# Who issues the blanking of one block of result rows: SyncE in place of ScalarE

## The reference

```
proj = x @ w_in
...
mix = jnp.concatenate([y_pool, y_conv], axis=-1) @ w_out
x = layer_norm(DEEPNORM_ALPHA_3 * x + mix, ln1_g, ln1_b)
ffn = moe(x, router_w, router_b, w_gate_up, b_gate_up, w_down, b_down)
```

## Time and profile before

| | before |
|---|---|
| median of 3 runs | 3319.97 us (3319.68 to 3324.28) |
| the profiled execution | 3321.52 us |
| its span, first to last instruction | 3319.7 us |
| TensorE busy | 94% of the span |
| VectorE, ScalarE, GpSimd busy | 55%, 48%, 22% |
| bytes moved | 693.72 MB, 209 GB/s over the span |
| the mixer stage | about 1800 to 1948 us |

### The profile page before, as it was taken

One profiled execution on the slowest core, in us unless ns is written; L12 is line 12 of the kernel. 1 busy time (PEld: TensorE's weight loads), 2 busy tenths in 40 slices (PEclk: granted clock), 3 DMA queues, 4 the chain that ended last, 5 costly groups with the idle time before them and its releaser, 6 DMA issues. The chain is left out here.

```text
span 3319.7 us, 39152 instructions
## 1 busy us (share of the span) xinstructions
PE 3104.9 (94%) x14036; PEld 2408.6 (73%) x14036; DVE 1830.9 (55%) x2216; ACT 1596.4 (48%) x2141; POOL 737.2 (22%) x379
## 2 busy tenths in 40 slices
PE   7986999998999999989997888999999999999997
PEld 6754678877877787768885666777777777777753
DVE  3257433344367404440031447887888888888773
ACT  4334434433566423232231325766766766666652
POOL 2400144442523344324442330000000000000020
PEclk9987999999999999999998898999999999999998
DMA  3243322222222132212224317999999999999971
GB/s 148 102 161 119 127 76 101 101 89 89 77 76 76 52 114 77 102 51 101 89 108 191 153 51 318 402 408 411 406 407 412 405 408 411 406 407 411 411 262 45
DMA packets 65594, 693.72 MB, mean 209 GB/s; under 512 B 6912, under 2 KB 7296, under 8 KB 25440
## 3 DMA queue, kind: packets, MB, share of 16 engines
q1 hardware_dynamic: 54336, 650.05, 49.8%
q0 software_dynamic: 6912, 25.17, 2.0%
q10 hardware_dynamic: 4256, 17.30, 1.3%
HBM read 654.22 MB, written 38.27 MB: 209 GB/s over the span
## 5 line engine op out<-in xcount | busy, mean ns | idle before, releaser
L142 POOL TENSOR_TENSOR ring_low<-ring,mix_ring_high 128x1024 fp32r<-128x1024 f32 x120 | 292.4, 2470 | 455.2 <-ACT mix_ring_high L137 455.2
L213 PE MATMUL psum<-mix_high,mix_ring_high 128*128 128x512 f32 x864 | 342.9, 397 | 13.1 <-DVE h_low L507 8.6
L215 PE MATMUL psum<-mix_high,ring_low 128*128 128x512 f32 x864 | 337.1, 390 | 0.0
L213 PE MATMUL psum<-ex_high,ex_rows_high 128*128 128x512 f32 x768 | 314.9, 410 | 1.5 <-DVE ex_rows_low L2823 1.4
L215 PE MATMUL psum<-ex_high,ex_rows_low 128*128 128x512 f32 x768 | 299.7, 390 | 0.0
L214 PE MATMUL psum<-h_low,mix_ring_high 128*128 128x512 f32 x736 | 287.2, 390 | 0.0
L142 POOL TENSOR_TENSOR ring_low<-ring,ff_ring_high 128x1024 fp32r<-128x1024 f32 x72 | 175.0, 2464 | 415.0 <-ACT ff_ring_high L137 224.7
L2510 POOL CAST ex_index<-table 128x1 uint32 (+1 forms) x32 | 5.9, 184 | 1090.2 <-PE psum L2550 1032.5
L2854 DVE TENSOR_TENSOR ring_low<-ring,ex_high 128x2048 fp32r<-128x2048 f32 x96 | 214.4, 2287 | 38.7 <-ACT ex_high L2686 38.6
L2854 DVE TENSOR_TENSOR ex_more_low<-ex_more,ex_high_in_x 128x2048 fp32r<-128x2048 f32 x96 | 219.5, 2287 | 19.9 <-ACT ex_high_in_x L2686 19.9
L2605 PE MATMUL psum<-ex_more,ex_act_t 128*128 128x512 f32 x512 | 224.9, 592 | 0.0
(11 more groups left out here) (581 smaller groups left out, 6884.8 us busy)
## 6 DMA issues: line engine op xcount, KB each, us to landing
ex_more<-moe_w SPq DMA_DIRECT2D x128, 2048.0 KB, 9.3
ring<-wstream SPq DMA_DIRECT2D x87, 2048.0 KB, 8.4
ring<-moe_w SPq DMA_DIRECT2D x64, 2048.0 KB, 10.5
ex_bias_up<-moe_b SPq DMA_DIRECT2D x32, 1024.0 KB, 9.6
y_rows<-mx_zero ACTq DMA_DIRECT2D x1, 16384.0 KB, 44.5
y_rows<-ex_y SPq DMA_DIRECT2D x32, 512.0 KB, 10.5
x<-xt SPq DMA_DIRECT2D x8, 256.0 KB, 6.1
rel<-rel_bias SPq DMA_DIRECT2D x1, 2048.0 KB, 9.7
```

The lines of the kernel that those rows point to most:

```text
L142: e.tensor_tensor(low, full, high.bitcast(F32), ALU.subtract).then_inc(self.low_ready, 1)
L213: pe.matmul(out, a[0], b[0], start=start, stop=False)
L215: return pe.matmul(out, a[1], b[0], start=False, stop=stop)
```

## The change

The issue of the small blanking leaves ScalarE's program. SP's program issues it, after its last ring load of the stage and behind a wait for the memset. SP's wait for both transfers at the end stays.

```diff
@@ mixer_stage, SP's program
                 g.clear_past(sp)
                 sp.dma_start(pool_mix[:, :, :], g.extra["pool_mix"]).then_inc(mix_in, 16)
                 ring.load_until(sp, min(n0 + 4 + SLOTS, FIRST["ple_proj"]))
+                sp.wait_ge(zeroed, 1)
+                sp.dma_start(r.y_dram[0:ROWS, :], zero[:, :]).then_inc(r.blanked, 16)
                 sp.wait_ge(r.blanked, 32)
@@ mixer_stage, ScalarE's program
                 first, count = S * TOPE // ROWS + 1, TABLE - S * TOPE // ROWS
                 act.dma_start(r.y_dram[first * ROWS:(first + count) * ROWS, :].rearrange("(b p) d -> p b d", p=ROWS),
                                zero[:, :].rearrange("p (a d) -> p a d", a=1).to_broadcast([P, count, D])).then_inc(r.blanked, 16)
-                act.dma_start(r.y_dram[0:ROWS, :], zero[:, :]).then_inc(r.blanked, 16)
                 norm.preload(act)
                 norm.root(act)
```

## The result

The first comparison gave 3295.22 us (median, 3292.19 to 3296.22) against 3319.97, a ratio of 0.9921 with a 95% interval of 0.9904 to 0.9938. The three gains between medians are 24.8, 32.1 and 30.8 us, each with an interval clear of no change; the prediction was 30.9. The profiled execution after took 3292.19 us, its span is 3290.4.

The account below looks back on a forecast made before the run. ScalarE, held 31.86 us at the small blanking's issue, was taken to stall the norm and TensorE. 31.32 - 0.42 (turns) + 0 (clock) - 0 (stage end) - 0 (contention) = 30.9 us off the median 3319.97: 3289.1 us, range 3286.5 to 3296.0.

Parts of the forecast that it names:

- The path: Start of the mixer stage: ScalarE's table load follows the large issue at once, the norm's root comes 31.32 us earlier.
- The turns: TensorE's two groups of eight turns after the norm become one of sixteen in 3.51 us, taking 0.42 off the gain.
- The clock: TensorE's clock at the stage's first products: between 1.55 us more gain and 1.05 us less, taken as 0.
- The end of the stage: SP's small blanking lands after 10.5 us, covered by 1.7 us before GpSimd's last work ends; cost 0.
- Contention: Panel n0+2, now loaded while the large blanking still runs, may slip 8.8 us; cost taken as 0.
- C: Rival: whatever stands behind the large blanking on ScalarE is held, so the time stays 3320.0 us; chance 0.07.
- D: Rival: only an ordinary issue on ScalarE is saved, 0.46 us, giving 3319.5 us; chance 0.03.
- B: Rival: the small blanking on SP or panel n0+2 lands late, 3292.9 us, with the panel's cost 3294.9; chance 0.08.
- E: Rival, slower: SP meets what ScalarE met, the small blanking lands 46.2 us after its issue, 3323.1 us; chance 0.02.
- A: The forecast itself, 3289.1 us, spanning 3287.5 to 3290.6; chance 0.78.

Follow-up runs that it names:

- the kernel with 16 blocks: Kernel before, ScalarE's order kept, but its large blanking has 16 blocks instead of 32 and SP issues the other 16; 3304.47 us against 3321.39.
- the one with 8 blocks: Kernel before, ScalarE's order kept, but its large blanking has 8 blocks instead of 32 and SP issues the other 24; 3298.05 us against 3321.39.

## Why the prediction was right

**The path.** The removed issue had held the table load, and the load followed the large issue at once. The root came 0.26 us behind the start of the variance instruction (1805.00 to 1805.26), as predicted.

**The turns.** Sixteen in a row took 3.79 us, not the 3.51 of the earlier norm; this is the term that was mis-sized, by 0.28 us. It is nearly the whole difference between the predicted 30.9 us and the 30.68 us that VectorE's low part moved.

**The clock.** The prediction took nothing. TensorE began its products at half speed again at 1813.13; the granted clock was 0.50 from 1813 to 1815 and 0.68 from 1815 to 1817, so it rose near 1816.3, 3.2 us after the first product, against 3.1 before. The term is zero here. That it would be was a choice between two rows and not derived; the kernel with 16 blocks, where the clock rose only 6.0 us after the first product, shows that it could have cost something.

**The end of the stage.** The landing price, 10.9 us against the 10.5 taken from the expert stage's stores, was right, and the cover 1.3 us instead of 1.7. Five blocks in place of one showed what it costs without cover: 3.65 us.

**Contention.** Panel n0+2 was issued at 1836.65 and in ScalarE's hands at 1847.31, 10.7 us later instead of 8.3: a slip of 2.4 us inside a cover read as 8.8. So the landing did slip, against what the prediction took from the row of pool_mix; the cover made it cost nothing. TensorE did not notice (0.82 us idle ahead of the panel in both kernels). The blanking in turn landed 50.2 us after its issue instead of 44.5, which nobody waits for.

**The rivals.** C, that whatever stands behind the large blanking is held, fell with the table load 0.04 us behind it in the changed kernel; D fell with the size of the gain, and with the swapped order, in which ScalarE keeps both issues and the stage is as short as after the change. B was kept away by covers of one and several us; five blocks on SP, and the late panel n0+3, used them up and cost 3.65 and 4.8 us. In the second, 1.7 us of that are the clock's, a price that the prediction did not put on a late panel. E did not come because SP had too little of its own ahead of the small blanking; with 24 blocks ahead, SP was held 4.99 us. Of the rule of the Trainium skill cited against the change ("DMA: Bandwidth & Descriptors", "Issuing engines are not separate DMA queues"), the "usually small" fits each of the 0.4 us issues here; it doesn't fit an issue behind 16 MB on the same engine.

**The size in time.** The first comparison gave 6 us less than the sum. The stage itself gave 30.7, as its length in five profiles shows, and two further comparisons gave 32.1 and 30.8; the 6 us are taken for scatter between executions. The first median, 3295.22, lies only 0.8 us under the upper bound of the forecast's range, 3296.0. That bound had been set for a late landing (B), which did not happen, so it was luck that it took in this scatter. The later medians, 3289.94 and 3290.79, lie 0.8 and 1.7 us above the forecast of 3289.1, within what A alone spans or 0.2 us over it.

## What to carry to other kernels

An engine that computes should not issue a transfer behind a very large one of its own: here the second issue held the engine until some 12 us before the first had landed, for 4 KB as for 512 KB. Issue the small one first, or from another engine; the first costs one exchanged line, and its stage was as short as that of the change. In a profile, look for DMA issues with a long duration of their own: an engine held there counts as idle, and the instruction behind it shows the gap as "issue". And before an issue is moved to the end of a stage, read what still runs there: here 1.3 us of cover was left, and four blocks more used it up and cost 3.65.

## What the runs showed of the hardware

- The issue of a 16 MB blanking is over in 0.46 us, but a second one from the same engine is held until 12.2 us before the first lands (12.3 with 16 blocks ahead). With 32 blocks of 512 KB ahead it was held 31.9, 31.5 and (4 KB) 31.7 us, with 16 blocks 12.0 us, with 8 blocks 0.6 us.
- The limit belongs to the issuing engine: SP, issuing 2.3 us behind ScalarE's 16 MB, was held 1.32 us; SP behind 12 MB of its own, 21.4 us later, 4.99 us. Whether the room that runs out is counted in bytes or in rows (each row here is 4 KB) wasn't tried.
- A blanking of 127 rows, alone on the DMA engines, moved at 26 GB/s and was through some 28 us after its issue; one of 128 rows landed after 10.9 us, behind a panel.
- In the kernel before and the changed one the granted clock rose from 0.50 to 1.00 of full speed 3.1 and 3.2 us after the stage's first product; in the kernel with 16 blocks, 6.0 us after it. In the one with 8 blocks, behind a wait of 3.96 us, it was 0.51 from 1887.5 to 1891.
